# Second buffer for the masked value block and a new order of issue in the decode state update

## The reference

```python
def step(R, xs):
    qc, kc, vc = xs
    scores = jnp.einsum('bhid,bhjd->bhij', qc, kc) * decay[None]
    o = jnp.einsum('bhij,bhjv->bhiv', scores, vc)
    o = o + jnp.einsum('bhid,bhdv->bhiv', qc, R) * xi[None, :, :, None]
    R_new = R * g_chunk[None, :, None, None] + jnp.einsum(
        'bhjd,bhjv->bhdv', kc * zeta[None, :, :, None], vc)
    return R_new, o
```

## Time and profile before

| what | value |
|---|---|
| median of 2 runs | 1285.63 us (1284.55 to 1286.71) |
| the profiled execution, slowest core | 1278.79 us, of which the span is 1277.2 us (core 7) |
| spans of the other cores | 1257.2 to 1275.4 us |
| TensorE, busy share of the span | 73% |
| VectorE | 37% |
| ScalarE | 15% |
| GpSimd | 9% |
| mean granted TensorE clock, core 7 | 0.868 of full |
| HBM traffic over the span | 179 GB/s |

### The profile page before, as it was taken

The page is one execution under the profiler, slowest core; times in us unless marked ns, Lnnn a source line. Parts: engine busy times, 40 slices in busy tenths (PEclk is TensorE's granted clock), DMA queues, the critical chain, the costliest instruction groups (busy, mean ns, idle before and its releaser), DMA issues.

```text
span 1277.2 us, 14511 instructions; the slowest of 8 cores (1257.2 to 1277.2 us)
## 1 busy us (share of the span) xinstructions
PE 928.6 (73%) x4586; PEld 444.7 (35%) x4586; DVE 477.6 (37%) x1076; ACT 197.1 (15%) x393; POOL 119.9 (9%) x143
## 2 busy tenths in 40 slices
PE   0337433578888796998879699797976765769875
PEld 0113122233433343444434344343433432424343
DVE  1442455344245544425544342453442222212321
ACT  1002121000222211121321102122211000001110
POOL 1001110110000011210001111000111100100100
PEclk9968766688989898999989899898988777779889
DMA  4998889899999313753331375223127334342461
GB/s 83 173 209 102 132 121 208 99 237 187 203 172 234 122 51 129 237 193 115 111 123 43 122 232 196 76 108 132 59 81 264 100 117 121 118 133 99 181 235 45
DMA packets 90393, 182.17 MB, mean 143 GB/s; under 512 B 17288, under 2 KB 62992, under 8 KB 79440
## 3 DMA queue, kind: packets, MB, share of 16 engines
q1 hardware_dynamic: 43376, 145.86, 35.2%
q0 software_dynamic: 46944, 35.40, 20.2%
HBM read 194.54 MB, written 34.41 MB: 179 GB/s over the span
## 4 chain that ended last, share of the span: by engine, by line
PE 53%; DMA 16%; DVE 13%; issue 7%; another core or an unknown queue 5%; ACT 2%; POOL 2%; DVEq 1%; SPq 1%; ACTq 0%; POOLq 0%
PE pb L878 18%; PE pb L896 12%; DMA arena<-wscratch 9%; PE pb L819 5%; PE pb L555 5%; PE pb L634 5%; DMA wscratch<-w_in 4%; PE pb L852 2%; PE ptb L509 1%; ACT arena L500 1%; PE pb L747 1%; DVE arena L804 1%; POOL arena L474 1%; DVE arena L783 1%
## 5 line engine op out<-in xcount | busy, mean ns | idle before, releaser
L878 PE MATMUL pb<-arena 128*128 128x512 bf16 x1408 | 354.6, 407 | 49.5 <-DMA arena<-wscratch 40.0
L878 PEld LDWEIGHTS pb<-arena 128*128 128x128 bf16 x1408 | 143.0, 104 | 239.3 <-issue 105.8
L896 PE MATMUL pb<-arena 128*128 128x512 bf16 x748 | 170.8, 389 | 12.1 <-DVE arena L886 6.0
L634 PE MATMUL pb<-arena 128*128 128x512 bf16 (+1 forms) x480 | 112.5, 386 | 27.6 <-DMA arena<-wscratch 19.5
L509 PE MATMUL ptb<-arena 128*128 128x128 bf16 x272 | 28.3, 267 | 132.8 <-DVE arena L543 68.8
L555 PE MATMUL pb<-arena 128*128 128x512 bf16 x408 | 105.0, 413 | 24.7 <-DMA arena<-wscratch 24.7
L886 DVE TENSOR_TENSOR arena<-pb,arena 128x512 bf16<-128x512 f32 x88 | 60.4, 689 | 150.2 <-PE pb L878 140.3
L896 PEld LDWEIGHTS pb<-arena 128*128 128x128 bf16 x748 | 74.1, 100 | 102.8 <-issue 21.4
L883 ACT ACTIVATE arena<-pb 128x512 bf16<-128x512 f32 x88 | 52.1, 596 | 372.6 <-PE pb L878 368.5
L500 ACT ACTIVATE arena<-arena 128x1024 bf16<-128x1024 f32 x51 | 53.8, 1055 | 283.7 <-DVE arena L823 139.3
L474 POOL TENSOR_TENSOR arena<-arena 128x1 f32<-128x1 f32 (+1 forms) x50 | 32.7, 654 | 535.7 <-DVE arena L503 297.3
(11 more groups left out here) (92 smaller groups left out, 700.8 us busy)
## 6 DMA issues: line engine op xcount, KB each, us to landing
arena<-wscratch SPq DMA_DIRECT2D x85, 1024.0 KB, 7.0
arena<-x SPq DMA_DIRECT2D x34, 512.0 KB, 5.1
arena<-wscratch SPq DMA_DIRECT2D x20, 768.0 KB, 5.2
arena<-tabs SPq DMA_DIRECT2D x34, 384.0 KB, 7.3
y<-arena POOLq DMA_DIRECT2D x16, 512.0 KB, 3.0
wscratch<-w_gate POOLq DMA_DIRECT2D x11, 512.0 KB, 13.4
wscratch<-w_up POOLq DMA_DIRECT2D x11, 512.0 KB, 8.4
arena<-w_down POOLq DMA_DIRECT2D x1, 5632.0 KB, 66.0
```

The lines of the kernel that those rows point to most:

```text
L634: P.group(pe, [lambda e, kc=kc: e.matmul(bk[:, 0:N], lhsT=panv[:, kc, k * 128:(k + 1) * 128], rhs=h1T[:, kc, 0:N], start=(kc == 0), stop=( ...
L878: P.group(pe, [lambda e, kc=kc: e.matmul(bk[:, 0:N], lhsT=panv[:, kc, t, fl * 128:(fl + 1) * 128], rhs=h2T[:, kc, 0:N], start=(kc == 0), s ...
L896: P.group(pe, [lambda e, fc=fc: e.matmul(bk[:, :], lhsT=aT[:, fc, s * 128:(s + 1) * 128], rhs=wdn[:, fc, half * 512:(half + 1) * 512], sta ...
```

## The change

A second buffer for the masked values is laid over `ra`, and the two are used by turns (`Vb`). `mk_vblk(0)` and `ld_rf(0)` stand ahead of the loop; in iteration i, `mk_vblk(i+1)` is issued after the key matmuls, and `ld_rf(i+1)` right behind the store of iteration i, before the yield. Both key matmuls are issued before VectorE's part. The yield's first number becomes 1.0 instead of 0.6.

```diff
--- before.py
+++ after.py
@@ -739,35 +739,55 @@
                 HB = DEC_PER // 2
                 P.op(act, lambda e: e.activation(out=qf, in_=qkT[:, 0:4, :], func=AF.Copy),
                      reads=[qkTB], writes=[qfB])
-                for h in range(4):
-                    for hf in range(2):
-                        b0 = hf * HB
-                        P.dma(sp, lambda e: e.dma_start(
-                            out=Rf, in_=sr_d[b0:b0 + HB, h, :, :].rearrange("b d v -> d b v")), d_rf, writes=[RfB])
-                        P.group(pe, [lambda e, bl=bl: e.matmul(
-                            XTv[:, h, (b0 + bl) * DEC_SEQ:(b0 + bl + 1) * DEC_SEQ], lhsT=Rf[:, bl, :],
-                            rhs=qf[:, h, (b0 + bl) * DEC_SEQ:(b0 + bl + 1) * DEC_SEQ], start=True, stop=True)
-                            for bl in range(HB)],
-                            reads=[RfB, qfB, STB], writes=[bankB[BS]])
-                        P.op(dve if use_dve[0] else pool, lambda e: e.tensor_tensor(
-                            out=Vblk, in0=v_tok[:, s, h * 128:(h + 1) * 128].unsqueeze(1).to_broadcast([128, HB, 128]),
-                            in1=m1c[:, b0:b0 + HB].unsqueeze(2).to_broadcast([128, HB, 128]), op=ALU.mult),
-                            reads=[vB[s], constB], writes=[VblkB])
-                        P.op(dve, lambda e: e.tensor_scalar(out=Rf, in0=Rf, scalar1=float(gC[h]), scalar2=None,
-                                                            op0=ALU.mult), reads=[RfB], writes=[RfB])
-                        for q4 in range(2):
-                            bk, bkB = next_bank()
-                            P.op(pe, lambda e: e.matmul(
-                                bk[:, :], lhsT=qk_tok[:, s, 1, h * 128:(h + 1) * 128],
-                                rhs=Vblk[:, 4 * q4:4 * q4 + 4, :], start=True, stop=True),
-                                reads=[qkB[s][1], VblkB], writes=[bkB])
-                            P.op(dve, lambda e: e.scalar_tensor_tensor(
-                                out=Rf[:, 4 * q4:4 * q4 + 4, :], in0=bk[:, :].rearrange("p (b v) -> p b v", b=4),
-                                scalar=float(gC[h]), in1=Rf[:, 4 * q4:4 * q4 + 4, :], op0=ALU.mult, op1=ALU.add),
-                                reads=[bkB, RfB], writes=[RfB])
-                        P.dma(sp, lambda e: e.dma_start(
-                            out=rets_d[b0:b0 + HB, h, :, :].rearrange("b d v -> d b v"), in_=Rf), d_rs, reads=[RfB])
-                        yield (0.6, 8.0)
+                Vb = [(Vblk, VblkB), (ra.bitcast(BF16).rearrange("p (b v) -> p b v", b=HB), raB)]
+                its = [(h, hf) for h in range(4) for hf in range(2)]
+
+                def mk_vblk(i):
+                    h_, hf_ = its[i]
+                    vb, vbB = Vb[i % 2]
+                    P.op(dve if use_dve[0] else pool, lambda e: e.tensor_tensor(
+                        out=vb, in0=v_tok[:, s, h_ * 128:(h_ + 1) * 128].unsqueeze(1).to_broadcast([128, HB, 128]),
+                        in1=m1c[:, hf_ * HB:(hf_ + 1) * HB].unsqueeze(2).to_broadcast([128, HB, 128]), op=ALU.mult),
+                        reads=[vB[s], constB], writes=[vbB])
+
+                def ld_rf(i):
+                    h_, hf_ = its[i]
+                    P.dma(sp, lambda e: e.dma_start(
+                        out=Rf, in_=sr_d[hf_ * HB:(hf_ + 1) * HB, h_, :, :].rearrange("b d v -> d b v")),
+                        d_rf, writes=[RfB])
+
+                mk_vblk(0)
+                ld_rf(0)
+                for i, (h, hf) in enumerate(its):
+                    b0 = hf * HB
+                    vb, vbB = Vb[i % 2]
+                    P.group(pe, [lambda e, bl=bl: e.matmul(
+                        XTv[:, h, (b0 + bl) * DEC_SEQ:(b0 + bl + 1) * DEC_SEQ], lhsT=Rf[:, bl, :],
+                        rhs=qf[:, h, (b0 + bl) * DEC_SEQ:(b0 + bl + 1) * DEC_SEQ], start=True, stop=True)
+                        for bl in range(HB)],
+                        reads=[RfB, qfB, STB], writes=[bankB[BS]])
+                    bk2 = [next_bank(), next_bank()]
+                    for q4 in range(2):
+                        bk, bkB = bk2[q4]
+                        P.op(pe, lambda e: e.matmul(
+                            bk[:, :], lhsT=qk_tok[:, s, 1, h * 128:(h + 1) * 128],
+                            rhs=vb[:, 4 * q4:4 * q4 + 4, :], start=True, stop=True),
+                            reads=[qkB[s][1], vbB], writes=[bkB])
+                    if i + 1 < len(its):
+                        mk_vblk(i + 1)
+                    P.op(dve, lambda e: e.tensor_scalar(out=Rf, in0=Rf, scalar1=float(gC[h]), scalar2=None,
+                                                        op0=ALU.mult), reads=[RfB], writes=[RfB])
+                    for q4 in range(2):
+                        bk, bkB = bk2[q4]
+                        P.op(dve, lambda e: e.scalar_tensor_tensor(
+                            out=Rf[:, 4 * q4:4 * q4 + 4, :], in0=bk[:, :].rearrange("p (b v) -> p b v", b=4),
+                            scalar=float(gC[h]), in1=Rf[:, 4 * q4:4 * q4 + 4, :], op0=ALU.mult, op1=ALU.add),
+                            reads=[bkB, RfB], writes=[RfB])
+                    P.dma(sp, lambda e: e.dma_start(
+                        out=rets_d[b0:b0 + HB, h, :, :].rearrange("b d v -> d b v"), in_=Rf), d_rs, reads=[RfB])
+                    if i + 1 < len(its):
+                        ld_rf(i + 1)
+                    yield (1.0, 8.0)
                 P.op(act, lambda e: e.activation(out=ra, in_=banks[BS][:, :], func=AF.Copy),
                      reads=[bankB[BS]], writes=[raB])
                 fns = []
```

## The result

| | before | changed |
|---|---|---|
| median | 1285.67 us (10 runs) | 1306.0 us (11 runs) |
| ratio | 1 | 1.0135, 95% interval 1.0095 to 1.0174 |
| span of the profiled execution, slowest core | 1277.2 us | 1307.9 us (core 3) |
| spans of the other cores | 1257.2 to 1275.4 us | 1276.5 to 1295.7 us |
| first to last state store, mean of the cores | 134.3 us | 152.3 us |

The changed kernel is 1.35% slower, 17 us of 1286, with an interval from 12 to 22. The medians differ by 20: on eight cores some executions of the same kernel are disturbed and run up to 9% longer, and the ratio leaves those out.

The account below looks back on a forecast made before the run. TensorE waits for weight panels queued on SyncE behind stores that wait for VectorE. Delays of 12.0 + 2.3 + 1.2 + 0.3 = +15.8 us on the median of 1285.63 give 1301.4, say 1302 us, range 1287 to 1315.

Parts of the forecast that it names:

- The second buffer and the new order: GpSimd's earlier multiplications into two blocks and the reordered key matmuls: cost 0, gain 0, since TensorE never waits for GpSimd.
- The load's place: State load moved right behind the store on SyncE, ahead of the panel: the part that costs, +15.8 us in sum.
- i = 1: Behind this iteration's store, load and store stood together already: nothing moves, 0.
- The hold: SyncE's state load waits for the store's landing, so the panel starts 3.84 us behind the store instead of 0.54, 3.30 later.
- The bytes ahead of the panel: The state load's 512 KB ahead of the panel in the same queue: 0.7 us taken, between 0 and 1.10.
- The sum without this term: If later descriptors overtook at every store, the bytes term would be 0 and the sum about 13 us.
- i = 3, 4 and 6: Panels behind these stores, all waited for at once: 3.3 + 0.7 = 4.0 us each, 12.0 together.
- i = 2 and i = 5: Panels behind these stores start 1.6 and 2.0 us later; with the bytes and slack they cost 2.3 and 1.2 us.
- rival B: Slower by over 2%: delays at their upper ends plus 5 us from TensorE's lower clock at i = 5, 1315 us; chance 0.14.
- i = 0: Behind this store the convolution's store waited for VectorE anyway: only bytes, 0.3 us.
- A: Nothing is lost: panel landings are set by other cores' traffic, not by their issue; 1284 to 1289 us, chance 0.10.
- C: Faster: TensorE's full clock returns sooner after longer waits, up to 29 us; 1282 us if it gives 20, chance 0.06.

Follow-up runs that it names:

- second profile of before: The kernel before, unchanged, profiled once more: 137.4 us from first to last state store, where its first profile gave 134.3 us.
- hold-only kernel: The kernel before with SyncE made to wait for each state store's landing, the load keeping its late place: ratio 1.0053, 142.8 us from first to last store.

## Why the prediction was right, point by point

The forecast was 1302 us, +16, within 1287 to 1315; measured 1306.0 as a median and +17 by the ratio.

*The second buffer and the new order are worth nothing.* Right. The load put back gives 0.998 with 1 inside its interval, and a block of four times the cost gives 1.000. A gain of up to 0.5% isn't excluded by the first interval (0.9949 to 1.0010).

*The load's place is the whole cost.* Right: 1.0126 for it alone, and 14.9 us in six intervals. The interval behind i = 1 was to stay and showed only what it also does in other executions of before.

*The hold.* The issue was to be 3.84 us behind the store instead of 0.54, and is (3.84, mean of 24).

*The bytes ahead of the panel.* This term was mis-sized: taken at +0.7, it is -0.3 (a landing of 6.26 us instead of 6.53; -0.5 against the second profile of before). Its bound of 1.1 was about right for a panel alone (1.05 measured against the hold-only kernel, 1.3 behind i = 3). The sum without this term, given as about 13, is 9.9 + 1.6 + 0.5 = 12.0 by the prediction's own numbers. What the step left out is that the panel of before shared its flight with the store just issued, which costs 1.3, and that a held panel no longer does. So i = 3, 4 and 6 cost 3.0 us each at the panel's landing, and 3.1, 3.4 and 2.7 in the intervals, not 4.0: 9.1 instead of 12.0.

*i = 2 and i = 5.* Both were too small: 3.2 instead of 2.3, and 2.6 instead of 1.2. At i = 2 the 3.65 us from store to panel were core 7's, the longest of the eight; their mean is 3.11, and 6.01 in the changed kernel. That is 2.9 later and not 1.6. At i = 5 the new wait came as foreseen (2.93 us on core 3). The panel was issued 4.86 us behind the store instead of the 4.34 worked out, mostly because the store there landed later; over the cores it went from 2.12 to 5.05, again 2.9 later and not 2.0. And part of rival B came true: the 16 matmuls behind the wait took 5.13 us instead of 3.5. The rows, core 3:

```profile
1127.56 6.43 PE L898 MATMUL pb<-arena 128*128 128x512 bf16 x24
1136.92 5.13 PE L898 MATMUL pb<-arena 128*128 128x512 bf16 x16 [2.93 <-DMA arena<-wscratch]
```

So the sum of 15.8 was met by 14.9 in the loop through errors of opposite sign, 2.9 us too much at i = 3, 4 and 6 and 0.3 at i = 0, 2.3 too little here. The mechanism was right; that the number came so close is in part luck. The remaining 2 or 3 us of the total are within its interval, and nothing here tells whether they are the changed kernel's; the longer interval behind i = 1 (13.5 against 12.3 to 15.7 in kernels without the change) is no evidence for it.

*The rivals.* A (nothing lost) falls with the runs above. B's clock came in part: from first to last store TensorE was busy 90.0 us in the changed kernel and 89.0 in the old one with the load moved, mean of the cores, against 85.9 to 87.3 in the four kernels whose load stands in its old place. So some 2.7 of the 14.9 us are slower matmuls and not waiting (roughly: the ends of matmuls are modelled); the rows above show 1.7 us of it at i = 5 on core 3. C (the clock gives time back): the granted clock from first to last store, mean of the cores, is 0.70 in those two and 0.72 to 0.73 in those four. It fell, so nothing was given back.

What the prediction saw and didn't use is the larger matter. It said that SyncE is on the path "each time its program stands at a store, waiting for VectorE". What follows from that sentence is worth 5.6%, over four times what the change lost.

## What to carry to other kernels

When an engine waits for another for 119 us, look for the opposite wait before giving it a second buffer: a buffer helps only where its consumer waits for its producer. In this kernel, the queue that issues prefetches in program order should hold nothing that waits for a compute engine or for a landing. Read it by asking, at each DMA with a semaphore, what stands behind it, and price a move by the issue time of what is behind, not by the size of what is moved: here 16 KB stores held as much as 512 KB ones. When you test whether one engine disturbs another, look at all of the other's instructions: the one line watched here was the one that wasn't hit. Transfers in flight together slow each other, so measure hold and bytes together; they don't add.

## What was not expected of the hardware

- A 1 MB panel landed in 5.2 us with neither state store nor load ahead of it, in 6.1 to 6.3 behind a 512 KB load, in 6.5 to 6.8 beside a 512 KB store to HBM, and in 7.3 beside both.
- While GpSimd ran its multiplications of some 2 us, some of VectorE's instructions stood still: one of 0.29 us took up to 1.98, one of 0.41 up to 2.02 and a copy of 0.17 up to 1.83. The scaling (started before GpSimd) and the additions of a PSUM bank to the state (L765), which ran beside it, took what they always take.
- A state store landed in 3.3 us, or in 4.5 to 6.5, at the same place of the program, on one core and not on its neighbour; the interval of the loop behind it is then mostly 3 to 5 us longer.
- Issued by GpSimd, the state's transfers landed in 5.0 (load) and 4.3 us (store) at the median of core 1, by ScalarE in 3.9 and 3.2 on core 5; the issue on GpSimd took 0.9 us instead of 0.4. GpSimd's queue was the better place all the same.
